# A transformer pair with a mixture of experts on one core: the prefetch issued by SyncE, expert weights in units that hold slices of both experts, and the last stage by halves

## The reference, cut to what matters

```python
gates = jax.nn.sigmoid((n @ w_gate[l] + b_gate[l]).astype(jnp.float32)).astype(n.dtype)
...
merged = (gates[:, :, 0] * (y_a @ w_branch[l, 0])
          + gates[:, :, 1] * (y_b @ w_branch[l, 1])
          + gates[:, :, 2] * (y_m @ w_branch[l, 2]))
h = h + merged @ w_out[l]
h = h + hier_moe(rmsnorm(h, g_ffn[l]), w_group[l], b_group[l], w_sub[l], b_sub[l], w1[l], w3[l], w2[l])
...
for e in range(N_EXPERTS):
    hid = jax.nn.silu(t @ w1[e]) * (t @ w3[e])
    out = out + combine[:, e:e + 1] * (hid @ w2[e]).astype(jnp.float32)
...
return rmsnorm(h, g_final)
```

## Time and profile before

| | us |
|---|---|
| median of 3 runs | 1133.74 |
| lowest, highest | 1132.47, 1136.60 |
| the profiled execution | 1130.59 |
| its span, first to last instruction | 1128.8 |
| TensorE busy | 1051.3 |
| VectorE busy | 400.3 |
| ScalarE busy | 333.1 |

### The profile page before, as it was taken

One profiled execution on the slowest core, in us unless ns is written; L12 is line 12 of the kernel. 1 busy time (PEld: TensorE's weight loads), 2 busy tenths in 40 slices (PEclk: granted clock), 3 DMA queues, 4 the chain that ended last, 5 costly groups with the idle time before them and its releaser, 6 DMA issues.

```text
span 1128.8 us, 13342 instructions
## 1 busy us (share of the span) xinstructions
PE 1051.3 (93%) x4960; PEld 669.1 (59%) x4960; DVE 400.3 (35%) x1181; ACT 333.1 (30%) x781; POOL 13.7 (1%) x60
## 2 busy tenths in 40 slices
PE   3899999999979998999999999898999999999985
PEld 0344554444457766768888557677888854444432
DVE  2349264332258554622842004741112320100004
ACT  3222143332043345224454014642001321111112
POOL 0000000000000000000000000000000000000010
PEclk9999999999989999999999999998999999999998
DMA  9997217352233212443444442019544779999995
GB/s 369 380 349 252 75 37 302 151 219 75 74 137 125 78 72 84 182 150 112 150 150 149 149 149 79 35 65 423 222 149 191 275 295 419 421 421 423 422 421 213
DMA packets 32908, 238.20 MB, mean 211 GB/s; under 512 B 3696, under 2 KB 3952, under 8 KB 6768
## 3 DMA queue, kind: packets, MB, share of 16 engines
q1 hardware_dynamic: 28192, 200.29, 45.6%
q10 hardware_dynamic: 4080, 34.99, 8.1%
q0 software_dynamic: 576, 2.10, 0.5%
HBM read 232.65 MB, written 19.40 MB: 223 GB/s over the span
## 4 chain that ended last, share of the span: by engine, by line
PE 86%; DMA 6%; ACT 3%; DVE 2%; issue 1%; ACTq 1%; SPq 0%; DVEq 0%
PE lin L457 29%; PE aux L457 9%; PE lin L828 9%; PE lin L539 8%; PE sc L480 6%; PE aux L828 4%; PE aux L742 4%; DMA ring<-w_stream 3%; PE sc L575 3%; DMA PR<-w_stream 3%; PE sc L796 3%; PE aux L603 3%; PE lin L589 2%; PE sc L510 1%; PE lin L549 1%
## 5 line engine op out<-in xcount | busy, mean ns | idle before, releaser
L457 PE MATMUL lin<-H,ring 128*128 128x256 f32 (+1 forms) x1360 | 340.8, 412 | 5.7 <-ACT H L1044 3.8
L457 PEld LDWEIGHTS lin<-H,ring 128*128 128x128 f32 x1360 | 260.9, 193 | 82.9 <-issue 48.1
L539 PE MATMUL lin<-ring,H 128*128 128x512 f32 (+2 forms) x256 | 90.1, 513 | 0.0
L457 PE MATMUL aux<-Y,ring 128*128 128x512 f32 (+1 forms) x256 | 84.0, 487 | 5.4 <-DVE Y L1434 4.1
L457 PEld LDWEIGHTS aux<-Y,ring 128*128 128x128 f32 x256 | 48.2, 190 | 40.3 <-issue 31.0
L539 PEld LDWEIGHTS lin<-ring,H 128*128 128x128 f32 x256 | 46.3, 190 | 42.7 <-issue 30.1
L480 PE MATMUL sc<-H,ring 128*128 128x512 f32 (+1 forms) x192 | 70.8, 503 | 0.0
L992 ACT ACTIVATE SP<-lin 128x512 f32<-128x512 f32 (+3 forms) x96 | 43.8, 468 | 85.1 <-PE lin L589 85.0
L1382 DVE SCALAR_TENSOR_TENSOR UN<-UN,cols 128x512 f32<-128x512 f32 (+1 forms) x120 | 64.5, 610 | 0.0
L955 ACT ACTIVATE NB<-lin 32x256 f32<-32x256 f32 x168 | 63.0, 375 | 2.6 <-DVE PR L1300 0.6
L510 PE MATMUL sc<-ring,CW 128*32 128x512 f32 x192 | 27.9, 705 | 24.9 <-DMA ring<-w_stream 24.9
(11 more groups left out here) (269 smaller groups left out, 1180.4 us busy)
## 6 DMA issues: line engine op xcount, KB each, us to landing
ring<-w_stream SPq DMA_DIRECT2D x127, 1024.0 KB, 5.2
SP<-w_stream SPq DMA_DIRECT2D x12, 1024.0 KB, 24.8
Y<-w_stream SPq DMA_DIRECT2D x8, 1024.0 KB, 17.8
UN<-w_stream SPq DMA_DIRECT2D x8, 1024.0 KB, 22.9
PR<-w_stream SPq DMA_DIRECT2D x8, 1024.0 KB, 26.5
X<-w_stream SPq DMA_DIRECT2D x7, 1024.0 KB, 21.6
CW<-w_stream SPq DMA_DIRECT2D x6, 1024.0 KB, 23.0
H<-w_stream SPq DMA_DIRECT2D x4, 1024.0 KB, 21.5
```

The source lines that it names most:

```text
L457: m = mm(dst, w[:, k, :], rhs(k), start=n == 0, stop=n == KT - 1)
L539: m = mm(bank[:, 0:width], src[:, k, tt * P:(tt + 1) * P], w[k // 4][:, k % 4, 0:width], start=k == 0, stop=k == KT - 1)
```

## The change

It has three parts.

1. SyncE issues the 11 prefetched units instead of ScalarE. TensorE's program notes (`turn["prefetch"]`) up to which unit the ring is filled when the attention ends, which is unit 90: `at["block"]` is 169 there, so half of unit 84 and the units 85 to 89 are left in the ring. SyncE loads up to that unit, waits for the last attended product as ScalarE did, issues the 11 units, and goes on with the ring.
2. A unit of expert weights holds two slices (k) of both experts instead of four of one (`couple_of` in place of `rows_of`). `both` waits for one unit for four matmuls, two k times two experts, and frees it behind them.
3. In the last pair the low half is scattered between the two units of `aux[0]`, added, multiplied with the gain, and its sum of squares prepared, before VectorE copies the high half. At the end only the high half is left; ScalarE multiplies the low half with the reciprocal, VectorE the high one; SyncE stores two pieces of 128x1024 in place of four.

```diff
                     gate(*divmod(n, 3))
                 if mp == 0:
+                    turn["prefetch"] = at["block"] // UNIT + SLOTS
...
-                def both(bank, left, n_k, j0, done):
-
-                    for half in range(n_k // 4):
-                        w = [unit(j0 + 2 * half + x) for x in range(2)]
-                        for k in range(4):
+                def both(bank, left, n_k, j0, done, between=None):
+
+                    for j in range(n_k // 2):
+                        w = unit(j0 + j)
+                        for k in (2 * j, 2 * j + 1):
                             for x in range(2):
                                 c = slice(x * CAP, (x + 1) * CAP)
-                                last = 4 * half + k == n_k - 1
-                                m = mm(bank[c, :], left[:, 4 * half + k, c], w[x][:, k, :], start=half + k == 0, stop=last)
-                                if k == 3 and not (last and x == 1):
+                                m = mm(bank[c, :], left[:, k, c], w[:, k % 2 * 2 + x, :], start=k == 0, stop=k == n_k - 1)
+                                if x == 0 or k % 2 == 0:
+                                    frees(m)
+                                elif k < n_k - 1:
                                     m.then_inc(unit_free, 1)
-                                elif k < 3:
-                                    frees(m)
+                        if between and j == 0:
+                            between()
                     at["owed"] += 1
                     m.then_inc(done, 1)
...
-                both(aux[0], HT, 4, 10, e_y)
+                both(aux[0], HT, 4, 10, e_y, scattered_lo if last else None)
+
+            def scattered(half):
+
+                for tt in range(TT):
+                    mm(sc[:, tt, half * 512:(half + 1) * 512], SWT[:, tt * P:(tt + 1) * P], YS[:, half * 512:(half + 1) * 512],
+                       start=True, stop=True).then_inc(e_out, 1)
+
+            def scattered_lo():
+
+                pe.wait_ge(e_swt_in, 1)
+                pe.wait_ge(e_y_lo, last_pair + 1)
+                scattered(0)
             for i in range(PAIRS - 2):
...
                 experts(late + (PAIRS - 2), late)
             experts(last_pair, turns, last=True)
-            pe.wait_ge(e_swt_in, 1)
-            for half, stored in enumerate((e_y_lo, e_y_hi)):
-                pe.wait_ge(stored, last_pair + 1)
-                for tt in range(TT):
-                    mm(sc[:, tt, half * 512:(half + 1) * 512], SWT[:, tt * P:(tt + 1) * P], YS[:, half * 512:(half + 1) * 512],
-                       start=True, stop=True).then_inc(e_out, 1)
+            pe.wait_ge(e_y_hi, last_pair + 1)
+            scattered(1)
...
                 sp.dma_start(X[:, :, half, :], x_in[:, :, half, :]).then_inc(x_in_s[n], 16)
             for slot in range(SLOTS):
                 load(slot, slot)
-            with sp.Fori(1, head // SLOTS) as r:
+            full = turn["prefetch"] // SLOTS
+            with sp.Fori(1, full) as r:
+                for slot in range(SLOTS):
+                    sp.wait_ge(unit_free, SLOTS * r + slot - SLOTS + 1)
+                    load(SLOTS * r + slot, slot)
+            for u in range(SLOTS * full, turn["prefetch"]):
+                sp.wait_ge(unit_free, u - SLOTS + 1)
+                load(u, u % SLOTS)
+            sp.wait_ge(aux_ready, V_TURN[first["abm"] + len(STAGES["abm"]) - 1] + 1)
+            for n in range(RING_AT - 2):
+                sp.dma_start(ASIDE[n], w_stream[BASE + n].rearrange("p b n -> p (b n)")).then_inc(aside_in[n], 16)
+            again = turn["prefetch"] // SLOTS + 1
+            for u in range(turn["prefetch"], min(head, SLOTS * again)):
+                sp.wait_ge(unit_free, u - SLOTS + 1)
+                load(u, u % SLOTS)
+            with sp.Fori(again, head // SLOTS) as r:
                 for slot in range(SLOTS):
...
                 sp.wait_ge(unit_free, BASE + PAIR_UNITS * (last_pair - 1) + n - AGAIN + 1)
                 load_expert(BASE + n, n)
-            for n in range(2 * TT):
-                sp.wait_ge(finished, n + 1)
-                c = slice(n % 2 * 512, n % 2 * 512 + 512)
-                sp.dma_start(out[n // 2, :, c], XT[:, n // 2, c]).then_inc(out_s, 16)
-            sp.wait_ge(out_s, 2 * TT * 16)
+            for tt in range(TT):
+                sp.wait_ge(finished, tt + 1)
+                sp.wait_ge(finished_lo, tt + 1)
+                sp.dma_start(out[tt], XT[:, tt, :]).then_inc(out_s, 16)
+            sp.wait_ge(out_s, TT * 16)
...
-            act.wait_ge(aux_ready, V_TURN[first["abm"] + len(STAGES["abm"]) - 1] + 1)
-            for n in range(RING_AT - 2):
-                act.dma_start(ASIDE[n], w_stream[BASE + n].rearrange("p b n -> p (b n)")).then_inc(aside_in[n], 16)
             act.wait_ge(lin_taken, turn["gate", *divmod(EARLY - 1, 3)] + 1)
...
@@ -1188,7 +1212,12 @@
                     fn(YG[half][:, tt * 512:(tt + 1) * 512], XT[:, tt, c], ACT.Square, accum_out=SS[:, half, tt:tt + 1]).then_inc(squared, 1)
             for tt in range(TT):
                 act.wait_ge(f_scale, tt + 1)
-                fn(SS[:, 3, tt:tt + 1], SS[:, 2, tt:tt + 1], ACT.Sqrt, bias=col("eps"), scale=1.0 / D).then_inc(f_rms, 1)
+                act.wait_ge(squared, TT + tt + 1)
+                fn(SS[:, 3, tt:tt + 1], SS[:, 1, tt:tt + 1], ACT.Sqrt, bias=SS[:, 2, tt:tt + 1], scale=1.0 / D).then_inc(f_rms, 1)
+            for tt in range(TT):
+                act.wait_ge(f_inverse, tt + 1)
+                act.wait_ge(gained, tt + 1)
+                fn(XT[:, tt, 0:512], XG[:, tt, :], ACT.Copy, scale=RV[:, 0, tt:tt + 1]).then_inc(finished_lo, 1)
...
+            def added(half):
+
+                for tt in range(TT):
+                    c = slice(half * 512, half * 512 + 512)
+                    dve.wait_ge(e_out, half * TT + tt + 1)
+                    v.tensor_tensor(XT[:, tt, c], sc[:, tt, c], XT[:, tt, c], ALU.add).then_inc(summed, 1)
+
...
+                    after(at["step"])
+                    added(0)
+                    dve.wait_ge(gain_in, 16)
+                    for tt in range(TT):
+                        dve.wait_ge(summed, tt + 1)
+                        v.tensor_tensor(XG[:, tt, :], XT[:, tt, 0:512], GAIN[:, 0:512], ALU.mult).then_inc(gained, 1)
+                    for tt in range(TT):
+                        dve.wait_ge(squared, tt + 1)
+                        v.tensor_scalar(SS[:, 2, tt:tt + 1], SS[:, 0, tt:tt + 1], 1.0 / D, EPS, ALU.mult, ALU.add).then_inc(f_scale, 1)
                 dve.wait_ge(e_y, 2 * i + 2)
                 dve.wait_ge(rows_stored, 16 * i + 1)
                 v.tensor_copy(YS[:, 512:1024], aux[0][:, :]).then_inc(e_y_hi, 1)
...
             experts(last_pair, last=True)
-            after(at["step"])
-            for half in range(2):
-                for tt in range(TT):
-                    c = slice(half * 512, half * 512 + 512)
-                    dve.wait_ge(e_out, half * TT + tt + 1)
-                    v.tensor_tensor(XT[:, tt, c], sc[:, tt, c], XT[:, tt, c], ALU.add).then_inc(summed, 1)
-            dve.wait_ge(gain_in, 16)
-            for tt in range(TT):
-                dve.wait_ge(squared, TT + tt + 1)
-                v.tensor_tensor(SS[:, 2, tt:tt + 1], SS[:, 0, tt:tt + 1], SS[:, 1, tt:tt + 1], ALU.add).then_inc(f_scale, 1)
+            added(1)
             for tt in range(TT):
                 dve.wait_ge(f_rms, tt + 1)
-                after(step(v.reciprocal(RV[:, 0, tt:tt + 1], SS[:, 3, tt:tt + 1])))
-                for half in range(2):
-                    c = slice(half * 512, half * 512 + 512)
-                    v.scalar_tensor_tensor(out=XT[:, tt, c], in0=XT[:, tt, c], scalar=RV[:, 0, tt:tt + 1], in1=GAIN[:, c],
-                                           op0=ALU.mult, op1=ALU.mult).then_inc(finished, 1)
+                v.reciprocal(RV[:, 0, tt:tt + 1], SS[:, 3, tt:tt + 1]).then_inc(f_inverse, 1)
+            for tt in range(TT):
+                dve.wait_ge(f_inverse, tt + 1)
+                dve.wait_ge(summed, TT + tt + 1)
+                v.scalar_tensor_tensor(out=XT[:, tt, 512:D], in0=XT[:, tt, 512:D], scalar=RV[:, 0, tt:tt + 1], in1=GAIN[:, 512:D],
+                                       op0=ALU.mult, op1=ALU.mult).then_inc(finished, 1)
...
-def rows_of(w):
-
-    return w.reshape(4, P, 512).transpose(1, 0, 2).reshape(P, 4 * 512)
+def couple_of(w):
+
+    n = w.shape[1] // (2 * P)
+    return w.reshape(2, n, 2, P, 512).transpose(1, 3, 2, 0, 4).reshape(n, P, 4 * 512)
...
     for e in range(0, N_EXP, 2):
-        for w in (a["w1_2"][0], a["w3_2"][0]):
-            tail += [rows_of(w[e + x, h * 512:(h + 1) * 512]) for h in range(2) for x in range(2)]
-        tail += [rows_of(a["w2_2"][0, e + x][:, n * 512:(n + 1) * 512]) for n in range(2) for x in range(2)]
-    w_stream = np.concatenate(head + [units(*stream), np.stack(tail)]).reshape(N_UNITS, P, UNIT, KT * P)
```

(3 more changed lines are left out.)

4 lines of the change are left out of this document (3 added, 1 removed).

## The result

The changed kernel takes 1126.65 us in the median of 5 runs (1124.06 to 1128.33), where the kernel before took 1133.74 (1130.43 to 1137.29, 5 runs beside it). The ratio is 0.9932, with a 95% interval of 0.9910 to 0.9955: 0.7% faster. The profiled execution took 1124.26 us with a span of 1122.4 us; before it was 1130.59 and 1128.8.

A forecast was written before the change was run, and what follows sets the result against it. The end was taken to hang on the last expert-weight unit's landing, any earlier TensorE delay moving it one for one; 6.6 us (part 1) plus 0.5 (parts 2 and 3) off 1133.7 gave 1126.6 us, range 1122 to 1132.

The forecast's parts named there:

- wait and clock together: Branch products behind the attention: TensorE's 3.9 us wait and 2.7 us of lowered clock both go, 6.6 us.
- the cover: Ring behind the prefetch: next unit lands at about 791, ring runs dry at 797, leaving 6 us.
- rival D: Ring behind the prefetch: it starves and TensorE waits; from no measurable change to 7.6 us slower, 1141; chance 0.05.
- Four matmuls fewer: End of expert stage: four matmuls instead of eight behind the last landing, 3.65 us becomes 1.83.
- The early release: Expert weight stream: places come free after four matmuls, 1.74 us earlier, so the last unit lands 1.7 us earlier.
- the queue on VectorE: Tail: gathered-row addition, two low sums, two gain products and two one-column operations precede the YS copy, ending at 1118.4.
- TensorE meanwhile stands still from 1114.1 to 1118.4, 4.3 us: Tail: TensorE idles before the high scatter, whose products then probably take 1.7 us each, not 0.9, at lowered clock.
- rival B: Tail: clock holds or gathers are ready earlier, shortening VectorE's queue; 8.5 up to 9.5 us gained, 1125 to 1124; chance 0.22.
- its signs of being wrong: TensorE waiting for a ring unit around 797, pair 0 later than 904, or last landing to end outside 14 to 16.5 us.
- 3.1 to 3.2: Final stores: time behind the work, from 2.5 us moving the last megabyte and a 1.4 us start beginning 0.7 earlier.
- Nearly all of what the earlier landing gives is used up here: Tail: VectorE's queue makes the YS copy end at 1118.4, against 1118.68 before.
- rival C: Branch products: the prefetch wait goes only partly, 3.3 + 0.5 to 3.9 + 0.5 us gained, 1129.6; chance 0.18.

The follow-up runs named there:

- p2_only: Kernel before with only the units holding slices of both experts, old prefetch and tail: median 1132.15 us, ratio 0.9989.
- act_late: Kernel before with ScalarE keeping the 11 prefetch issues but making them behind its eight early sigmoids: median 1127.94 us, ratio 0.9943.
- p12: Kernel before with SyncE's prefetch and the two-expert units, tail as before: median 1125.4 us, ratio 0.9922.
- p12_couples: p12 with the places of two units again freed together: median 1124.41 us, ratio 0.9919.
- stores4: Changed kernel with four final stores of 256 KB in place of two of 512 KB: median 1126.94 us, ratio 0.9931.
- couples_after: Changed kernel with the places of two units again freed together: median 1126.25 us, ratio 0.9942.
- copy_first: Changed kernel with VectorE's copy of the high half ahead of the gain products and one-column operations: median 1123.83 us, ratio 0.9917.
- tile_order: copy_first with the first token tile finished first on VectorE and ScalarE: median 1124.64 us, ratio 0.9917.

## Why the prediction was right

The predicted 1126.6 us stand against 1126.65, but two of the terms behind it were off in opposite directions. That the two agree to 0.05 us is luck: the interval of the ratio is 5.1 to 10.2 us of gain, and the profiled execution, forecast at 1123.5, took 1124.26.

**Part 1 held.** It was counted at 6.6 us, wait and clock together; measured are 6.85 in every kernel that has it, against the profile of before. Against p2_only, whose prefetch is ScalarE's as before, it is 5.7: the wait there is 3.85 again, but the 32 records behind it took 8.61 us instead of 9.69, so the clock's share is 1.6 to 2.7. act_late shows the mechanism. Pair 0 began at 903.59, not 902.4: in that execution the branch products began 0.58 us later and the routing took 0.84 longer, and 6.85 - 0.58 - 0.84 = 5.43 = 909.02 - 903.59. The ring unit landed at 792.6, where 791 was counted, and in this execution TensorE came to the block that needs it at 797.8 (one block behind the branch products that end at 794.31); the cover was 5.2 us rather than 6, and rival D never came near.

**Part 2 was under-counted on one side and over-counted on the other.** Four matmuls fewer gave 1.9 (counted 1.83). The early release, counted at 1.7, gave 1.0: the first reload went out 1.97 us behind pair 0, as said, but the last product starts at +203.9 in p12 where +205.0 in p12_couples. The stream itself moved by 1.5 (mean parts of the table); the rest is how the last parts fell. In the changed kernel the last unit landed at 1108.1 and not at 1105.7: pair 0 began 1.2 us later than counted, and from pair 0 on it landed at +204.5 where +203.3 was counted and +205.0 was measured before.

**Part 3: the queue on VectorE was right, two sizes behind it were not.** Its order and reason are as predicted: the gathered block at +204.22 (counted +204.32), then the queue, 2.57 us up to the copy where 3.1 were counted. The step that failed is **"TensorE meanwhile stands still from 1114.1 to 1118.4, 4.3 us"**. It took the low scatter as done at +203.3, and it was done at +204.8: the unit before the last came at +200.99, where +199.8 was counted, and the products behind it took 0.3 longer. The last product therefore began later, the gap was 2.11 us, the granted clock stayed at 1.00 and the scatter took 1.98 us. That was rival B's condition, and it left the arithmetic ending at +214.2, against +216.1 in the forecast and +214.6 at full clock. stores4 shows the predicted fall, behind a gap of 2.85: the mechanism exists, and did not act in this execution. So of what the prediction named as signs, the 4 us of idling and the 0.5 behind them did not come, while none of its signs of being wrong did: pair 0 began at 903.59 with 904 as the bound, and the last landing stood 14.3 us ahead of the end, with 14 as the bound.

The second is the term for the stores, **"3.1 to 3.2"** behind the work, measured 4.62. It counted 1.4 for the start, which no row shows and which measured 0.85, and 2.5 for the move, which took 2.9; it left out the completion, 1.5 us, of which 0.9 is the late part of the last store. The two errors, 1.9 gained and 1.5 lost, nearly cancel by luck, and the tail came out at 218.81 where 219.28 was forecast.

**What the single parts add up to.** The forecast has parts 2 and 3 together 0.5 us better than before; the profiled executions show 0.97. But p12 shows that part 2 alone gave 3.0, and that part 3 took 2.0 of it back. The account of part 3 from p12 to the changed kernel: copy 2.04 later, arithmetic behind it 2.20 shorter, stores 2.16 longer, 2.0 in sum. Of the 2.16, 0.9 is the late part of the last store; if that belongs to the execution and not to the new tail, which no run decides, part 3 cost 1.1. Shortening the arithmetic behind the copy had no net use, because it was shortened by finishing both halves of both tiles at the same time, so that the whole megabyte is stored at the end. Before, the first three of four stores were issued ahead of its end, and some 0.5 MB had moved by then (380 GB/s from 1125.00 to 1126.32). The prediction saw only that "Nearly all of what the earlier landing gives is used up here", not that the tail loses against leaving it alone. The pairs of profiles agree (p12 and changed 2.0, p12_couples and couples_after 1.6); their medians differ in the same direction, by 1.2 and 1.8 us, within their intervals. One slip in the working changes nothing in the forecast: rival C's "other way round", the clock won and not the wait, is 2.7 and not 3.3. copy_first, p12, p12_couples and tile_order, at 0.9917 to 0.9922, can't be told from one another, nor surely from the changed kernel's 0.9932.

## What to carry to other kernels

Issuing a transfer occupies the engine that issues it, here half a microsecond each, so put a burst of issues where the next operation on that engine is not waited for; which engine it is matters less. When a chain ends in a store, count three pieces for it (start, data that is not yet under way, completion), and judge a shorter arithmetic by how much output it leaves to the end. A landing counts when its last part is there: before a difference of a microsecond between two profiles is put down to an edit, look whether one of the 16 parts was late. When work is brought forward on the engine that also makes the last hand-over, put the hand-over first and the work behind it.
